# A hybrid decoder step on one core: the V/K stage in eight slices of two K tiles instead of four quarters of four, and four scale-2 weight chunks moved into the first out-projection group

## The chip, the cores and the metric

The kernel runs on one core of one Trainium2 chip. The metric is the device time of one execution in microseconds. Three runs of the kernel before gave 1495.02, 1496.38 and 1498.96 us, median 1496.38.

## The reference, cut to what matters

256 prompt tokens and 8 x 8 sample tokens, 320 in all, D = 2048. All in float32.

```
def mixer_inputs(x, shift, scale, g_pre, w_in, pos):
    h = rms_norm(x, g_pre) * (1.0 + scale) + shift
    z = h @ w_in                       # 2048 -> 4096, columns q | k | v | u
    ...
mp = ada_modulation(c_prompt, ...)     # silu(c) @ w_ada + b_ada -> shift, scale, gate (mixer), shift, scale, gate (MLP)
q, k, v, u = mixer_inputs(xp, mp[0], mp[1], g_pre_mix[l], w_in[l], pos_p)
attn = prompt_attention(q, k, v, pos_p, lam)
pooled = pool_mix(u, ...)
xp = mixer_output(xp, attn, pooled, mp[2], ...)   # x + gate * rms_norm([a | pooled] @ w_out, g_post)
xp = ffn_block(xp, mp[3], mp[4], mp[5], ...)      # the same sandwich around relu(h @ w1)^2 @ w2
```

The sample tokens pass through the same functions with their own modulation (one row for each of 8 sequences), a paged K/V cache of 256 positions and a pooling state.

## The kernel before, in words

Activations lie channel-major: 16 K tiles of 128 channels x 320 tokens. Every weight product is made in three passes of fp32r matmuls (h_hi with w_hi, h_lo with w_hi, h_hi with w_lo): ScalarE rounds a weight half chunk to w_hi (`hi_half`, L390), VectorE subtracts to get w_lo (`lo_half`, L782), TensorE multiplies. A product chunk is 48 matmuls of 128x320.

All weights come as one stream of 272 chunks of 1 MB (128 x 2048 floats), which SP loads in two halves each (L342) into a ring of four slots `raw`. A slot is free again when it has been used: for a product chunk when both halves of w_lo are made, for a modulation ("ada") chunk when its four small matmuls on TensorE (L1500, or L1515 for the later blocks) are done. SP waits for the slots in order, so a late slot also holds up the chunks behind it. The order of the stream and the places of product chunks in it are tables: DENSE has a product at places 2, 5, 8, 11 of 12, SUPER at 1, 3, 5, 7 of 8.

The modulation has 24 blocks of four ada chunks. A block is finished by a copy on ScalarE (`ada_copy`, L384), four transposes on TensorE (`ada_turn`, L1525) and two VectorE steps (`mod_add`, L761 and L764). Blocks 0 to 7 are scale and shift of the mixer, alternating, each for 4 K tiles. Blocks 12 and up are accumulated in parts (`ada_part_chunk`); the first of these parts, blocks 12 to 15, is the scale of the MLP (scale 2), turned by `mod_part`.

The order around the change is written out by hand, engine by engine, with semaphores. At the start TensorE takes block 0, the mean of squares and block 1, while ScalarE and VectorE make rstd, h (scaled, shifted), h_hi and h_lo of the first four K tiles; POOL does the scale and shift of the sample tokens (L1350, L1352). The V/K stage then has four quarters: quarter g multiplies K tiles 4g to 4g+3 with all 16 column tiles of v and k, four tiles to a chunk; each result is the sum over 4 K tiles in one of four PSUM banks, which VectorE adds to v_cm or k_cm (`sum_tiles`, L857). Between them stand the ada chunks of the next two blocks. Then come the Q and U products with attention beside them (`fill`), the sample attention, and the out projection: 16 product chunks, one ada chunk ahead of each (`super4`, L1538), with the evacuation, squares and gates on ScalarE and VectorE. Early in it POOL reloads x (L1443), 2.6 MB. The MLP follows.

## Time and profile before

| what | value |
|---|---|
| median of three runs | 1496.38 us |
| profiled execution | 1494.64 us, its span 1493.0 us |
| TensorE (PE) busy | 1446.6 us, 97% |
| VectorE (DVE) busy | 799.7 us, 54% |
| ScalarE (ACT) busy | 517.5 us, 35% |
| moved by DMA | 316.40 MB, mean 212 GB/s |
| V/K stage | 43.73 to 198.88 us |
| out projection, first product | 410.56 us |

Busy time is the time an engine has an instruction running; matmuls are pipelined, so each is shown as some 310 ns long though a new one starts about every 147. The chain of waits goes back from the last instruction to whatever released each step. PE is the matmul side of TensorE, PEld its weight loads. Times within the span count from its first instruction.

### The profile page before, as it was taken

How to read it: one execution, taken by the hardware profiler on the slowest of the kernel's cores; microseconds unless marked ns; L12 is line 12 of the kernel's file. 1: busy time of each engine (PE TensorE's matmuls, PEld its weight loads, DVE VectorE, ACT ScalarE, POOL GpSimd, SP SyncE). 2: the span in 40 equal slices, each digit the busy share in tenths (PEclk: the TensorE clock that was granted, in tenths of full speed). 3: DMA queues.
4: the chain of work that ended last, by engine and by line, in shares of the span. 5: the costliest groups of instructions: out<-in, count | busy, mean ns of one | idle time of the engine just before them, and what ended most of it. 6: DMA issues, size and time to landing. Idle time of an engine off the chain costs nothing.

```text
span 1493.0 us, 26969 instructions
## 1 busy us (share of the span) xinstructions
PE 1446.6 (97%) x10274; PEld 1313.3 (88%) x10274; DVE 799.7 (54%) x1258; ACT 517.5 (35%) x733; POOL 102.9 (7%) x177
## 2 busy tenths in 40 slices
PE   5999999999899998999999999999999999999996
PEld 1777777778588877999998999999999999999996
DVE  2655558856756568665334444333554344445554
ACT  2222233434456445333322333332333232333331
POOL 1000000067410000000000000000000000000002
PEclk9999999999999999999999999999999999999998
DMA  9999988889687777444445544445544444444431
GB/s 366 345 326 323 325 305 318 284 308 360 226 321 257 258 256 248 141 152 158 143 160 200 176 160 148 147 162 185 192 158 144 157 151 141 143 155 152 141 113 71
DMA packets 87880, 316.40 MB, mean 212 GB/s; under 512 B 12176, under 2 KB 12432, under 8 KB 87168
## 3 DMA queue, kind: packets, MB, share of 16 engines
q1 hardware_dynamic: 79200, 287.87, 56.1%
q0 software_dynamic: 5216, 22.51, 4.1%
q10 hardware_dynamic: 3392, 5.01, 0.9%
q8 instruction: 51, 0.84, 0.2%
q14 instruction: 21, 0.17, 0.0%
HBM read 309.56 MB, written 5.80 MB: 211 GB/s over the span
## 4 chain that ended last, share of the span: by engine, by line
PE 83%; DMA 6%; DVE 3%; POOL 2%; issue 2%; ACT 2%; POOLq 1%; SPq 0%; DVEq 0%; ACTq 0%
PE bank L1538 69%; PE bank L1609 7%; DMA raw<-in_stream 4%; PE bank L1500 3%; PE bank L1515 2%; DMA k_pages<-in_kc 1%; DMA pools_out<-u 1%; DMA pool_w<-in_w_pool 1%; ACT w_hi L390 1%; DVE w_lo L782 1%; PE bank L1861 1%; POOLq L1377 0%; POOL win L1396 0%; POOL win L1398 0%; ACT pair L639 0%
## 5 line engine op out<-in xcount | busy, mean ns | idle before, releaser
L390 ACT ACTIVATE w_hi<-raw 128x1024 fp32r<-128x1024 f32 x352 | 361.8, 1054 | 352.8 <-PE bank L1538 232.8
L782 DVE TENSOR_TENSOR w_lo<-raw,w_hi 128x1024 fp32r<-128x1024 f32 x352 | 419.6, 1225 | 117.1 <-ACT w_hi L390 114.9
L1538 PE MATMUL bank<-m_hi,w_hi 128*128 128x320 f32 x1280 | 397.4, 310 | 1.0 <-issue 0.6
L1538 PE MATMUL bank<-m_hi,w_lo 128*128 128x320 f32 x1280 | 395.5, 309 | 0.0
L1538 PE MATMUL bank<-m_lo,w_hi 128*128 128x320 f32 x1280 | 395.5, 309 | 0.0
L1538 PE MATMUL bank<-h_hi,w_hi 128*128 128x320 f32 x1216 | 379.2, 312 | 0.0
L1538 PE MATMUL bank<-h_hi,w_lo 128*128 128x320 f32 x1216 | 375.7, 309 | 0.0
L1538 PE MATMUL bank<-h_lo,w_hi 128*128 128x320 f32 x1216 | 375.7, 309 | 0.0
L1538 PEld LDWEIGHTS bank<-m_hi,w_hi 128*128 128x128 f32 x1280 | 240.3, 188 | 15.0 <-issue 15.0
L1538 PEld LDWEIGHTS bank<-h_hi,w_hi 128*128 128x128 f32 x1216 | 228.2, 188 | 23.2 <-issue 23.2
L1538 PEld LDWEIGHTS bank<-m_lo,w_hi 128*128 128x128 f32 x1280 | 240.3, 188 | 0.0
L1538 PEld LDWEIGHTS bank<-m_hi,w_lo 128*128 128x128 f32 x1280 | 240.3, 188 | 0.0
L1538 PEld LDWEIGHTS bank<-h_lo,w_hi 128*128 128x128 f32 x1216 | 228.3, 188 | 0.0
L1538 PEld LDWEIGHTS bank<-h_hi,w_lo 128*128 128x128 f32 x1216 | 228.3, 188 | 0.0
L1244 DVE TENSOR_TENSOR relu<-relu 128x320 f32<-128x320 f32 x62 | 30.5, 492 | 191.5 <-ACT relu L672 191.5
L672 ACT ACTIVATE relu<-bank 128x320 f32<-128x320 f32 x60 | 26.2, 437 | 292.4 <-PE bank L1538 292.4
L1259 DVE TENSOR_TENSOR back<-bank,back 128x320 f32 (+1 forms) x48 | 23.6, 491 | 171.7 <-PE bank L1538 171.7
L1609 PE MATMUL bank<-h_hi,w_hi 128*128 x256 | 83.0, 324 | 1.4 <-DVE v_cm L857 0.6
L1609 PE MATMUL bank<-h_hi,w_lo 128*128 x256 | 79.1, 309 | 0.0
L1609 PE MATMUL bank<-h_lo,w_hi 128*128 x256 | 79.0, 309 | 0.0
L1609 PEld LDWEIGHTS bank<-h_hi,w_hi 128*128 128x128 f32 x256 | 48.0, 188 | 29.4 <-issue 24.2
L1464 POOL TENSOR_TENSOR back<-back,rstd 128x640 f32<-128x640 f32 (+1 forms) x3 | 3.9, 1314 | 938.1 <-ACT rstd L715 938.1
(237 smaller groups left out, 1095.3 us busy)
## 6 DMA issues: line engine op xcount, KB each, us to landing
raw<-in_stream SPq DMA_DIRECT2D x544, 512.0 KB, 5.0
k_pages<-in_kc POOLq DMA_DIRECT2D x16, 512.0 KB, 9.3
v_pages<-in_vc POOLq DMA_DIRECT2D x16, 512.0 KB, 6.9
x<-in_x_cm ACTq DMA_DIRECT2D x1, 2560.0 KB, 12.2
x<-in_x_cm POOLq DMA_DIRECT2D x1, 2560.0 KB, 10.8
v_out<-v_cm POOLq DMA_DIRECT2D x1, 1280.0 KB, 9.5
k_out<-back POOLq DMA_DIRECT2D x1, 1280.0 KB, 10.2
y_out<-x SPq DMA_DIRECT2D x2, 640.0 KB, 3.0
```

Of the source, the lines that this page charges most:

```text
L390: act.activation(w_hi[2 * (j % 2) + h][:, :], raw[slot][:, h * 1024:(h + 1) * 1024], ACT.Copy).then_inc(hi_ready, 1)
L672: freed(act.activation(relu[j % 2][:, :], bank[j % 2][:, 0:T], ACT.Relu), j)
L782: dve.tensor_tensor(w_lo[q][:, :], raw[slot][:, h * 1024:(h + 1) * 1024], w_hi[q][:, :], ALU.subtract).then_inc(slot_used[slot], 1)
L1244: mine.then(dve.tensor_tensor(relu2[j % 2][:, :], up, up, ALU.mult))
L1259: dve.tensor_tensor(tile, bank[j % 2][:, 0:T], tile, ALU.add).then_inc(bank_free[j % 2], 1)
L1464: mine.then(pool.tensor_tensor(part, part, rstd[:, :].unsqueeze(1).to_broadcast([P, end - first, T]), ALU.mult))
L1500: last = pe.matmul(ADA[32 * kk:32 * kk + NSEQ, :], silu_c[:, 4 * a + kk, :], raw[slot][:, kk * 512:(kk + 1) * 512], start=(a == 0), stop=( ...
L1515: last = pe.matmul(ADA[32 * g:32 * g + NSEQ, :], silu_c[:, a, :], raw[slot][:, g * 512:(g + 1) * 512], start=start, stop=(a == KT - 1))
L1538: last = pe.matmul(bank[j % 2][:, 0:T], w[q][:, k * P:(k + 1) * P], v[:, 8 * h + k, :], start=(h == 0 and k == 0 and n == 0), stop=(h == 1 ...
L1609: last = pe.matmul(QUARTER_BANKS[2 * h + i][:, 0:T], w[q][:, (4 * i + k) * P:(4 * i + k + 1) * P], v[:, ds(4 * g + k, 1), :].rearrange("p ...
L1861: last = pe.matmul(FIRST_BANKS[i][:, 0:T], w[q][:, at_k:at_k + P], v[:, 4 * c + k, :], start=(c == 0 and k == 0 and n == 0), stop=(c == 3 ...
```

## The change

The V/K stage runs in 8 slices of two K tiles instead of 4 quarters of four. A product chunk now holds 2 K tiles of 8 column tiles, so each half chunk writes all four PSUM banks with sums over two K tiles, and VectorE adds 128 such sums instead of 64. An ada block 0 to 7 now holds the scale and the shift of the same two K tiles, so one block (four chunks) is enough for a slice; the place table is SLICED, with products at 0, 3, 6, 9 of 12. ScalarE applies scale and shift to the prompt tokens in one instruction for each K tile, where VectorE used two. x is loaded on SP's queue, in four parts ahead of the stream, instead of ScalarE's; the squares, the sums and their mean stand ahead of block 0 on TensorE. The ten `keep_clock` matmuls are gone. The stream begins with 4 ada chunks instead of 8; everything up to the out projection moves up by four ada chunks, and the first out-projection group takes 8 of them (DENSE): the last four of scale 2 and the first four of shift 2. `make_scale2` therefore stands behind the first out-projection evacuation on VectorE.

```diff
-STREAM = 8 + 12 * QUARTERS + 12 * Q_GROUPS + 8 * (U_GROUPS + OUT_GROUPS) + 36 * GROUPS
+SLICES = 2 * QUARTERS
+STREAM = 4 + 12 * (QUARTERS + Q_GROUPS + 1) + 8 * (U_GROUPS + OUT_GROUPS - 1) + 36 * GROUPS
+SLICED = [0, 3, 6, 9]
+SLICED_ADA = [[1, 2, 4, 5], [7, 8, 10, 11]]
 DENSE = [2, 5, 8, 11]
-DENSE_ADA = [[0, 1, 3, 4], [6, 7, 9, 10]]
+NORMED = [(0, 2), (2, 4), (4, 8), (8, 12), (12, 16)]
 SUPER = [1, 3, 5, 7]
...
     def quarter_use(g):
-        return 2 + 3 * g
+        return 1 + 3 * g
 
     def out_use(n):
-        return 2 + 3 * (QUARTERS + Q_GROUPS) + 2 * (U_GROUPS + n)
+        return quarter_use(QUARTERS + Q_GROUPS) + 2 * (U_GROUPS + n) + (1 if n else 0)
 
...
+        for g in range(4):
+            sp.dma_start(x[:, 4 * g:4 * g + 4, :], x_cm[:, 4 * g:4 * g + 4, :]).then_inc(x_loaded[g], 16)
...
-        act.dma_start(x[:, :, :], x_cm).then_inc(x_loaded, 16)
...
+        def slice_h(n):
+
+            act.wait_ge(gate_done, n + 1)
+            act.wait_ge(normed_s, normed_by(n))
+            act.wait_ge(mod_done, n + 2)
+            for k in range(2):
+                tile = normed[:, 2 * n + k, 0:NP_]
+                act.activation(tile, tile, ACT.Identity, bias=mod[:, n, 2 + k, 0:1], scale=gate[:, 2 * n + k, 0:1]).then_inc(
+                    prompt_mod, 1)
+            act.wait_ge(prompt_mod, 2 * n + 2)
+            act.wait_ge(sample_mod, n + 1)
+            act.activation(h_hi[:, 2 * n:2 * n + 2, :], normed[:, 2 * n:2 * n + 2, :], ACT.Copy).then_inc(h_hi_s, 1)
...
-        ada_copy(1, 1, 3)
+        hi_half(0, quarter_use(0), SLICED[0], 0, 0)
+        slice_h(0)
+        hi_half(0, quarter_use(0), SLICED[0], 0, 1)
...
+        for n in range(SLICES):
+            second, following = slice_chunks(n)
+            for h in range(2):
+                hi_half(*second, h)
+            ada_copy(n + 1, quarter_use(n // 2), SLICED_ADA[n % 2][3])
+            hi_half(*following, 0)
+            if n + 1 < SLICES:
+                slice_h(n + 1)
+            hi_half(*following, 1)
...
+        def slice_gate(n):
+
+            mod_add(n)
+            dve.wait_ge(mod_done, n + 2)
+            dve.scalar_tensor_tensor(gate[:, 2 * n:2 * n + 2, :], mod[:, n, 0:2, :], 1.0,
+                                     gain[:, G_PRE_MIX + 2 * n:G_PRE_MIX + 2 * n + 2].unsqueeze(2).to_broadcast([P, 2, NSEQ]),
                                      ALU.add, ALU.mult).then_inc(gate_done, 1)
...
         invert_root(0)
-        mod_add(0)
-        times_rstd(normed, x, 0).then_inc(normed_s, 1)
-        dve.wait_ge(normed_s, 1)
-        dve.wait_ge(mod_done, 2)
-        scale_quarter(0)
-        mod_add(1)
-        shift_quarter(0)
-        low_of_h(1, 0)
-        for h in range(2):
-            lo_half(0, quarter_use(0), DENSE[0], 0, h)
-        for g in range(1, 4):
-            times_rstd(normed, x, g).then_inc(normed_s, 1)
-        dve.wait_ge(normed_s, 4)
+        for first, end in NORMED[:3]:
+            times_rstd(first, end)
+        slice_gate(0)
+        lo_half(0, quarter_use(0), SLICED[0], 0, 0)
+        low_of_h(0)
+        lo_half(0, quarter_use(0), SLICED[0], 0, 1)
+        for first, end in NORMED[3:]:
+            times_rstd(first, end)
...
+        def sum_tiles(n, jj, h):
+            half = 4 * n + 2 * jj + h
+            for i in range(4):
+                if i < 3:
+                    dve.wait_ge(first_done, 3 * half + i + 1)
                 else:
+                    dve.wait_ge(half_free, half + 5)
+                tile = (v_cm, k_cm)[jj][:, 4 * h + i, :]
+                dve.tensor_tensor(tile, QUARTER_BANKS[i][:, 0:T], tile, ALU.add).then_inc(bank_free[i], 1)
...
+        for n in range(SLICES):
+            second, following = slice_chunks(n)
+            for h in range(2):
+                lo_half(*second, h)
+                sum_tiles(n, 0, h)
+            if n + 1 < SLICES:
+                slice_gate(n + 1)
+            else:
+                mod_add(n + 1)
+            lo_half(*following, 0)
+            sum_tiles(n, 1, 0)
+            if n + 1 < SLICES:
+                low_of_h(n + 1)
+            lo_half(*following, 1)
+            sum_tiles(n, 1, 1)
...
+        def make_scale2():
+            mod_part(0, out_use(0), DENSE[1] - 1)
+            dve.wait_ge(part_done, 1)
+            dve.scalar_tensor_tensor(scale2[:, :, :], mod_of(SCALE2), 1.0,
+                                     gain[:, G_PRE_FFN:G_PRE_FFN + KT].unsqueeze(2).to_broadcast([P, KT, NSEQ]),
+                                     ALU.add, ALU.mult).then_inc(gate_done, 1)
...
+                if 4 * t + j == 1:
+                    make_scale2()
...
+        def quarter(g, last):
             use = quarter_use(g)
-            for j in range(4):
-                if j:
-                    second_ada(g, use, j)
-                else:
-                    pe.wait_ge(h_ready, g + 1)
-                slot, u = use_of(use, DENSE[j])
-                for h in range(2):
-                    pe.wait_ge(slot_used[slot], 2 * u + (3 + h))
-                    q = 2 * (j % 2) + h
-                    for i in range(2):
-                        pe.wait_ge(bank_free[2 * h + i], 4 * g + (j + 1))
-                        for k in range(4):
-                            for n, (w, v) in enumerate(((w_hi, h_hi), (w_hi, h_lo), (w_lo, h_hi))):
-                                last = pe.matmul(QUARTER_BANKS[2 * h + i][:, 0:T], w[q][:, (4 * i + k) * P:(4 * i + k + 1) * P],
-                                                 v[:, ds(4 * g + k, 1), :].rearrange("p a t -> p (a t)"),
-                                                 start=(k == 0 and n == 0), stop=(k == 3 and n == 2))
-                        last.then_inc(half_free if i else first_done, 1)
-                        if j == 3 and h == 0 and i == 0:
-                            ada_turn(3 + 2 * g)
-                        if j == 3 and h == 1 and i == 0:
-                            second_ada(g + 1, use + 3, 0)
-                    if h == 0 and j < 3:
-                        first_ada(g, use, j + 1)
-                    elif h == 0:
-                        first_ada(g + 1, use + 3, 0)
-                if j == 1:
-                    ada_turn(2 + 2 * g)
+
+            def slice_tiles(i, jj, h, tiles):
+
+                j = 2 * i + jj
+                slot, u = use_of(use, SLICED[j])
+                q = 2 * (j % 2) + h
+                pe.wait_ge(slot_used[slot], 2 * u + (3 + h))
+                for b in tiles:
+                    pe.wait_ge(bank_free[b], 8 * g + (2 * j + h + 1))
+                    for k in range(2):
+                        for n, (w, v) in enumerate(((w_hi, h_hi), (w_hi, h_lo), (w_lo, h_hi))):
+                            last = pe.matmul(QUARTER_BANKS[b][:, 0:T], w[q][:, (2 * b + k) * P:(2 * b + k + 1) * P],
+                                             v[:, ds(4 * g + (2 * i + k), 1), :].rearrange("p a t -> p (a t)"),
+                                             start=(k == 0 and n == 0), stop=(k == 1 and n == 2))
+                    last.then_inc(first_done if b < 3 else half_free, 1)
+
+            for i in range(2):
+                nb, places = 2 * g + (i + 1), SLICED_ADA[i]
+                ada_chunk(nb, use, places[0], 0)
+                pe.wait_ge(h_ready, 2 * g + (i + 1))
+                slice_tiles(i, 0, 0, range(4))
+                ada_chunk(nb, use, places[1], 1)
+                ada_chunk(nb, use, places[2], 2)
+                slice_tiles(i, 0, 1, range(2))
+                ada_chunk(nb, use, places[3], 3)
+                slice_tiles(i, 0, 1, range(2, 4))
+                ada_turn(nb)
+                slice_tiles(i, 1, 0, range(4))
+                slice_tiles(i, 1, 1, range(2))
+                if last and i == 1:
+                    nb, place, a = fill_ada(0)[0][0]
+                    ada_chunk(nb, fill(0)[1], place, a)
+                slice_tiles(i, 1, 1, range(2, 4))
+
+        with pe.Fori(0, QUARTERS - 1) as g:
+            quarter(g, False)
+        quarter(QUARTERS - 1, True)
...
-        for t in range(OUT_GROUPS - 1):
+        for j in range(4):
+            for i in range(2):
+                k = 2 * j + i
+                ada_part_chunk(k // 4, out_use(0), DENSE[j] - 2 + i, (12 + k) % KT, k == 4)
+            for h in range(2):
+                product_half(*out_chunk(j), h, m_hi, m_lo, mix_wait)
+        for t in range(1, OUT_GROUPS - 1):
             super4(OUT_C4 + t, out_use(t), 1, 4 * t, m_hi, m_lo, mix_wait)
```

Three places in the order of the instructions. First TensorE, from the start up to the first product; raw are ada chunks, the number being the slot of the ring (49 to 52), squares and rstd belong to the mean. Before:

```order
L1500 MATMUL bank<-raw_52,silu_c 9x512 x4
L1485 MATMUL bank<-rstd,ones 128x320
L1525 MATMUL bank<-tab,ada_rows 128x128 x4
L1500 MATMUL bank<-raw_49,silu_c 9x512 x4
L1500 MATMUL bank<-raw_50,silu_c 9x512 x4
L1500 MATMUL bank<-raw_51,silu_c 9x512 x4
L1500 MATMUL bank<-raw_52,silu_c 9x512 x4
L1525 MATMUL bank<-tab,ada_rows 128x128 x4
L1500 MATMUL bank<-raw_49,silu_c 9x512 x4
L1500 MATMUL bank<-raw_50,silu_c 9x512 x4
L1490 MATMUL bank<-ones 128x128 x10
```

and now, up to the waits in front of the first product:

```order
L1486 MATMUL bank<-squares,ones 32x320 x16
L1493 MATMUL bank<-rstd,ones 128x320
L1508 MATMUL bank<-raw_49,silu_c 9x512 x4
L1508 MATMUL bank<-raw_50,silu_c 9x512 x4
L1508 MATMUL bank<-raw_51,silu_c 9x512 x4
L1508 MATMUL bank<-raw_52,silu_c 9x512 x4
L1533 MATMUL bank<-tab,ada_rows 128x128 x4
L1620 UNCONDITIONAL_BRANCH
L1620 ISA
L1507 ISA
L1508 MATMUL bank<-raw_50,silu_c 9x512 x4
L1605 REGISTER_ALU
```

Of the ten ada chunks in front of the first product five are left (four of block 0, one of block 1), and the mean stands first.

Second VectorE in the V/K stage; w_lo is half a product chunk, v_cm and back (its upper half is k_cm) take the sums. Before, from the second half of a quarter:

```order
L782 TENSOR_TENSOR w_lo_59<-raw_52,w_hi_55 128x1024
L782 TENSOR_TENSOR w_lo_60<-raw_52,w_hi_56 128x1024
L857 TENSOR_TENSOR back<-bank,back 128x320
L854 REGISTER_ALU
L857 TENSOR_TENSOR back<-bank,back 128x320 x2
L854 REGISTER_ALU
L857 TENSOR_TENSOR back<-bank,back 128x320
L815 ISA x2
L815 SCALAR_TENSOR_TENSOR gate<-mod,gain 128x36
L818 REGISTER_ALU
L820 ISA
L820 TENSOR_TENSOR normed<-normed,gate 128x4x256
```

and now, the first slice:

```order
L806 TENSOR_TENSOR w_lo_59<-raw_52,w_hi_55 128x1024
L864 TENSOR_TENSOR v_cm<-bank,v_cm 128x320 x4
L806 TENSOR_TENSOR w_lo_60<-raw_52,w_hi_56 128x1024
L864 TENSOR_TENSOR v_cm<-bank,v_cm 128x320 x4
L785 TENSOR_REDUCE mod<-bank 128x36
L788 TENSOR_TENSOR mod<-mod,ada_bias 128x36
L834 SCALAR_TENSOR_TENSOR gate<-mod,gain 128x18
L806 TENSOR_TENSOR w_lo_57<-raw_51,w_hi_53 128x1024
L864 TENSOR_TENSOR back<-bank,back 128x320 x4
L827 TENSOR_TENSOR h_lo<-normed,h_hi 128x640
L806 TENSOR_TENSOR w_lo_58<-raw_51,w_hi_54 128x1024
L864 TENSOR_TENSOR back<-bank,back 128x320 x4
```

Four sums stand behind each half of w_lo where two stood, and w_lo halves alternate with them; the two VectorE steps on normed in each quarter are gone.

Third TensorE where the out projection begins; u and pool_w belong to the pooling mixer, m_hi is the input of the out projection. Before:

```order
L1727 MATMUL bank<-back,ones 128x512
L1744 MATMUL bank<-u,pool_w 128x320 x12
L1515 MATMUL bank<-raw_49,silu_c 9x512 x4
L1538 MATMUL bank<-m_hi,w_hi_53 128x320
L1538 MATMUL bank<-m_lo,w_hi_53 128x320
L1538 MATMUL bank<-m_hi,w_lo_57 128x320
```

and now:

```order
L1727 MATMUL bank<-back,ones 128x512
L1744 MATMUL bank<-u,pool_w 128x320 x12
L1523 MATMUL bank<-raw_49,silu_c 9x512 x4
L1523 MATMUL bank<-raw_50,silu_c 9x512 x4
L1546 MATMUL bank<-m_hi,w_hi_53 128x320
L1546 MATMUL bank<-m_lo,w_hi_53 128x320
L1546 MATMUL bank<-m_hi,w_lo_57 128x320
```

Two ada chunks stand ahead of the first product chunk, which is the third chunk of its group instead of the second.

## Rows read from the trace of the kernel before

**Rows 1.** The page: busy time of TensorE, and the chain that ended last.
```profile
PE 1446.6 (97%) x10274; PEld 1313.3 (88%) x10274; DVE 799.7 (54%) x1258; ACT 517.5 (35%) x733; POOL 102.9 (7%) x177
...
PE 83%; DMA 6%; DVE 3%; POOL 2%; issue 2%; ACT 2%; POOLq 1%; SPq 0%; DVEq 0%; ACTq 0%
```

**Rows 2.** Stretches: length, busy us of each engine, granted clock, DMA share, GB/s.
```profile
0.00:20.00 20.00, 7.84 (x20) 1.07 (x22) 3.41 (x26) 6.53 (x7) 3.26 (x7) 1.00 0.87 328
20.00:43.70 23.70, 18.42 (x126) 6.73 (x122) 10.04 (x12) 6.71 (x8) 5.65 (x3) 1.00 1.03 409
...
43.73:198.88 155.15, 154.24 (x1058) 120.23 (x1059) 86.41 (x126) 41.86 (x43) 4.43 (x7) 1.00 0.94 327
```

**Rows 3.** Timeline 0 to 44 us: start, length, engine, line, what [idle before].
```profile
8.37 1.88 PE L1500 MATMUL bank<-raw,silu_c 128*9 128x512 f32 x4
...
8.47 0.17 ACT L364 ACTIVATE small<-bank 128x2 f32<-128x2 f32 x1 [2.50 <-PE bank L1563]
14.14 4.75 ACT L369 ACTIVATE squares<-x 128x1280 f32<-128x1280 f32 x4 [5.50 <-DMA x<-in_x_cm]
...
23.00 0.60 PE L1500 MATMUL bank<-raw,silu_c 128*9 128x512 f32 x2
...
23.84 0.44 ACT L373 ACTIVATE rstd<-bank 128x320 f32<-128x320 f32 x1 [4.95 <-PE bank L1478]
...
26.15 2.15 DVE L750 RECIPROCAL rstd<-rstd 128x320 f32<-128x320 f32 x1 [6.15 <-ACT rstd L378]
...
29.50 1.03 PE L1500 MATMUL bank<-raw,silu_c 128*9 128x512 f32 x4 [0.25 <-DMA raw<-in_stream]
...
35.76 0.60 ACT L384 ACTIVATE ada_rows<-bank 128x512 f32<-128x512 f32 x1 [9.15 <-PE bank L1500]
...
37.44 0.20 DVE L764 TENSOR_TENSOR mod<-mod,ada_bias 128x36 f32<-128x36 f32 x1
...
39.56 1.27 ACT L420 ACTIVATE h_hi<-normed 128x1280 fp32r<-128x1280 f32 x1 [3.20 <-POOL normed L1352]
...
40.86 1.49 DVE L809 TENSOR_TENSOR h_lo<-normed,h_hi 128x1280 fp32r<-128x1280 f32 x1 [1.96 <-ACT h_hi L420]
41.05 1.06 ACT L390 ACTIVATE w_hi<-raw 128x1024 fp32r<-128x1024 f32 x1 [0.22 <-DMA raw<-in_stream]
...
43.73 0.41 PE L1609 MATMUL bank<-h_hi,w_hi 128*128 x1 [0.47 <-DVE w_lo L782]
```

**Rows 4.** Timeline of POOL: one step beside VectorE, and the same step later.
```profile
30.59 1.74 POOL L1350 TENSOR_TENSOR normed<-normed,gate 128x256 f32<-128x256 f32 x1 [2.91 <-DVE gate L815]
...
73.96 0.72 POOL L1350 TENSOR_TENSOR normed<-normed,gate 128x256 f32<-128x256 f32 x1 [34.49 <-DVE gate L815]
```

**Rows 5.** Chain of waits, 80 to 125 us: start, length, what.
```profile
87.59 3.72 PE bank L1609 x24
91.30 0.97 PE bank L1500 x8
...
102.81 5.92 DMA raw<-in_stream
```

**Rows 6.** Chain of waits, 405 to 445 us, out projection.
```profile
410.56 7.27 PE bank L1538 x48
...
418.81 7.24 PE bank L1538 x48
```

**Rows 7.** Groups of the V/K stage: busy us, mean ns | idle before.
```profile
L782 DVE TENSOR_TENSOR w_lo<-raw,w_hi 128x1024 fp32r<-128x1024 f32 x32 | 39.1, 1224 | 59.0 <-ACT w_hi L390 58.8
...
L857 DVE TENSOR_TENSOR v_cm<-bank,v_cm 128x320 f32<-128x320 f32 x32 | 13.4, 480 | 0.0
```

**Rows 8.** Out projection: POOL's reload of x, SP's issues at 411.5, ScalarE's next w_hi.
```profile
409.85 0.60 POOL L1443 DMA_DIRECT2D x<-in_x_cm  x1 [9.61 <-issue]
...
L342 SPq DMA_DIRECT2D raw<-in_stream x2: 353/548/744, 411.5 to 412.4; - x2
...
423.56 1.06 ACT L390 ACTIVATE w_hi<-raw 128x1024 fp32r<-128x1024 f32 x1 [3.50 <-DMA raw<-in_stream]
```

More of the change, by code:

```diff
@@ L60 @@
 FFN_C4 = OUT_C4 + OUT_GROUPS
-BANK_LEAD = 4 * QUARTERS - 2 * Q_C4
+BANK_LEAD = 8 * QUARTERS - 2 * Q_C4
 U_ORDER = [6, 7, 4, 5, 2, 3, 0, 1]
@@ new lines, in times_rstd @@
+        def times_rstd(first, end):
+            dve.tensor_tensor(normed[:, first:end, :], x[:, first:end, :],
+                              rstd[:, :].unsqueeze(1).to_broadcast([P, end - first, T]), ALU.mult).then_inc(normed_s, 1)
+        invert_root(0)
+        for first, end in NORMED[:3]:
[6 more added lines that the diff above has]
+            times_rstd(first, end)
```

236 lines of the change are left out of this document (88 added, 148 removed).

## The prediction

> **What bounds the kernel now.** I read the page first, then busy time by stretch, the timeline of the first 44 us, the groups of lines of the V/K stage, and the chain of waits in that stage and in the out projection. TensorE is busy 97% of the span and is 83% of the chain that ended last [rows 1]. So time is won where TensorE stands idle, and lost where it gets more work or a new wait. In the stretch 20.00 to 43.70 the DMA engines are full at 409 GB/s; in the V/K stage, 43.73 to 198.88, TensorE is busy 154.24 of 155.15 us [rows 2]. So there are two regimes: a start in which TensorE waits for bytes and for the chain that makes h, and a stage in which it hardly waits at all (0.91 us).
>
> The start, step by step [rows 3]: ScalarE squares x from 14.14 to 18.89; the last half chunk of scale-and-shift block 0 lands at 23.00; the rstd chain (copy 23.84, square root, reciprocal) ends at 28.30; block 1 (the shift) is through TensorE only at 35.76; its values are in at 37.64; h_hi ends at 40.83, h_lo at 42.35; the first product chunk lands at 41.05, and the first product starts at 43.73, after its w_lo. The product needs both 8 modulation chunks and the eleventh chunk of the stream.
>
> **The start after the change.** Bytes first. x now goes first on SP's queue. The row at 29.50 [rows 3] is TensorE waiting for the first half of stream chunk 6 (counted from 0), so x, the tables and chunks 0 to 5 had landed one half chunk earlier: 0.524 MB at 409 GB/s is 1.28 us, so at 28.2. The same bytes are ahead of chunk 5 now. SP's first DMA waited for VectorE's memset before and x does not, which is worth up to 0.9 us: I place chunk 5 at about 27.4 and its four TensorE matmuls' end at 28.0. Chunk 3 comes at 22.2 instead of 23.0.
>
> The h chain: ScalarE is free at 8.64 and the four squares take 4.75 [rows 3], x lands by about 11, so they end at 13.4. Sums add about 0.9, and from copy to reciprocal it is 4.46 (23.84 to 28.30): 18.8. The first three times_rstd cover 2560 elements, at the 1.49 of 1280 that h_lo shows 3.0: 21.8, before block 0 is through. Block 0: the second half of chunk 3 at 22.2, ada matmuls 0.7, then copy, turn and mod_add 1.93 (35.71 to 37.64): 24.9, gate 0.25: 25.1. Then two ScalarE activations of 256 (0.45 each by the h_hi row's rate plus start-up), beside two POOL operations of half the size of the ones in [rows 4]; they cost 0.4 to 0.9 each, I take 1.5 for the pair: 26.6. h_hi of 640 is half of 1.27, h_lo half of 1.49: with starts 28.2. Both paths meet at about 28.2. I take 28.5 for the first product; ends 27 and 31. Gain **15.2** (12.7 to 16.7).
>
> A rule of the Trainium skill bears on the POOL pair: "SBUF — State Buffer", section "SBUF: two separate sides", says that GpSimd and VectorE's instructions with two SBUF inputs take one port pair in turns, the later one blocked for the whole instruction. Rows agree: the same POOL operation took 1.74 us started right behind a VectorE one, 0.72 otherwise [rows 4]. By it the pair waits behind w_lo (VectorE, 1.22) and the start would be 29.3, the gain 0.8 smaller; by the undisturbed rows it would be 27.9.
>
> **V/K stage.** TensorE's product work is the same: 768 matmuls, 16 chunks. Half chunks of 24 take 3.72 followed by 0.97 for an ada chunk [rows 5]; 48 in one piece take 7.24 [rows 6]; so 24 more matmuls are 3.52 and each change of kind costs 0.2. Before, 32 ada chunks stood singly; now a slice of two products has three groups (1, 2 and 1), so 8 changes fewer, −1.6. Between first product and first Q product there were 32 ada chunks, now 33 (31 of blocks 1 to 8 and 2 of block 9): +1.0. A slice is then 4x3.52+4x0.98+3x0.2+0.4 (turn) = 19.0 us.
>
> VectorE is the new risk. Each slice has 16 sums of 128x320 instead of 8 per two products: 16x0.48 and 4 w_lo x1.22 [rows 7], mod_add and gate 0.7, h_lo 0.75: 14.0 of 19.0 us. With a 0.2 wake-up for each sum it is 17.2. It holds; four banks take turns, a bank is wanted 2.6 us after its last matmul. The chain turn, mod_add, gate, two activations, h_hi, h_lo ends about 5 us after the turn, and TensorE has 7.2 us of the second product left: hidden with 2 us spare. The cost of sums if that cover is gone is in the rivals.
>
> The ring of four slots: chunks 0 and 3 of a slice are products, whose slot frees with the second w_lo. A second half issued at 102.81 landed at 108.73 [rows 5]; it leaves about 0.6 after the slot is free, and a first half lands 1.28 before it. So from a free slot it is about 5.2 us to the first half and 6.6 to the second. In a later slice the second w_lo ends about 1.3 before the slice's end, its successor lands 5.3 after the slice starts and is wanted at 5.6: zero waiting, barely. In the first slice VectorE makes the second w_lo at 29.6 (after h_lo), so chunk 8 lands at 36.3 and its matmuls end at 36.8; TensorE wants it at 28.5+3.7+1.0 = 33.2 and would be done at 34.2: a wait of **2.6**. The stage before had waits of 0.9. Sum of the stage: +1.0−1.6+2.6−0.9 = **+1.1** (0 to +8).
>
> Q and U stages: the same chunks in the same pattern, starting 14.1 us earlier; attention, POOL's pages and stores hang on the stage, not on the clock on the wall. 0 (−2 to +2).
>
> **Out projection.** Four ada chunks more stand in group 0: 4x0.98 = 3.9. Before, TensorE finished the only ada chunk ahead of the first product at 410.2 and began at 410.56, after m_lo [rows 6]; the second now fills that: 3.9−0.35 = **+3.6**. VectorE's make_scale2 (transpose, add, scale) moves behind the first evacuation: some 2 us of VectorE beside a 9.2 us product tile, hidden.
>
> The new wait: the pattern before was ada, product, ada, product, and the four slots held both first products when the stage began. Now it is ada, ada, product, ada, and the second product is chunk 5, whose slot frees only when the second ada chunk is used (411.3). At that moment POOL reloads the 2.6 MB of x (issued 409.85), and the chunk issued at the same time before, at 411.5, was readable by ScalarE only at 423.56 [rows 8]: 12 us. w_hi 1.06 and w_lo 1.22 make it 425.8. TensorE is ready at 411.3+7.2+0.2+1.95 = 420.8. Wait **+5.0** (0 to +6). Before, that landing hit the third product and cost nothing.
>
> **Sum:** −15.2+1.1+3.6+5.0 = −5.5. The profiled execution took 1494.64 (span 1493.0), the median of the runs is 1496.38, 1.7 above it; so 1489.1 on the profiled one's scale and **1490.9** as a median.
>
> **Rivals.** (a) The late second product costs nothing: x and the stream share differently and chunk 5 lands 5 us earlier. For it: 4.7 MB at 409 GB/s needs 11.5, so against it. −10.5: 1485.9.
> (b) VectorE, not TensorE, sets the V/K slices. For: 128 sums instead of 64, each between a TensorE finish and a bank that TensorE wants back, with w_lo and mod_add in front of them in program order. Against: 14.0 of 19.0. It is even at 0.7 us a slice (5.5/8); at 1.4 a slice (bank waits of 0.35 at each of the four halves) it costs 11.2: 1502.1, slower.
> (c) The ring runs late in every slice, since the margin is 0.3: about 1 us in 7 slices, +7: 1497.9. For: raw landings are what ScalarE waits for in this stage already; against: the load per slice is 15.4 of 19.0 us.
> (d) The start comes out at half rate. The first four records of an ada chunk take 1.88, those at 29.50 take 1.03 [rows 3], and the granted clock reads 1.00 in both stretches [rows 2], so only durations show that the early ones ran near half the rate (1.2 against 2.4 GHz), after a start without work. Between 22.9 and 28.2 TensorE would be busy about 2.1 of 5.3 us (half of chunk 3, a turn, chunk 5), less than in any stretch before, and the ten keep_clock matmuls are gone. The first half product would then take 7 instead of 3.5; 2.6 of that hides in the wait for chunk 8; the rest, and what follows at the low level, costs up to 4: 1494.9.
> The Trainium skill, "TensorE: Matmul & The Clock Gate", section "HAM oscillation — how this bites in real kernels", names this danger: too little matmul work puts the array back to half clock. By it the time is that of (d), without it that of the sum; the rows at the start of the trace agree that a low level exists.
>
> **Chances.** Forecast 0.45; (a) 0.15; (b) 0.12; (c) 0.13; (d) 0.15. 0.3% is 4.5 us, about what a measurement of this kernel tells from no change, so the line runs at 1491.9, close above the forecast. Six tenths of the forecast (0.27), (a) (0.15) and a piece of (c) and (d) where they cost almost nothing (0.07) are faster: 0.49. Same: the rest of the forecast (0.18), most of (d) (0.11) and part of (c) (0.07): 0.36. Slower, above 1500.9: (b) and the tail of (c): 0.15. Range 1484 to 1499.5, which leaves out the worst of (b) and little of (a).
>
> **What would show it.** First product at 28.5 in the timeline; a TensorE wait on the stream of about 2.6 us at 33 to 37; slices of 19.0 us with no VectorE sum as releaser; first Q product near 184.8; in the out projection a wait of 5 us before the second product with w_lo as releaser; x_scaled unchanged beside it. Wrong would be: waits on sums in every slice, first product after 31, or no wait at the second out product.

## The result, and the profile after

The changed kernel took 1508.91 us (median of 4 runs, 1503.69 to 1513.10) against 1496.18 us for the kernel before, a ratio of 1.0074 (95% interval 1.0043 to 1.0105). A second set of 9 runs gave 1507.49 us and 1.0065 (1.0049 to 1.0081). So it is slower by 0.7%, 10 to 13 us, where 5.5 us of gain were forecast, and outside the forecast's range. The profiled execution took 1503.69 us with a span of 1502.0 us, 9.05 us more than the profiled one of the kernel before. It is the fastest of its four runs, and the profiled one of the second set (1511.04 us) the slowest of its nine, so the two profiles stand at the two ends of what this kernel does.

The page of the changed kernel, busy time and the chain that ended last, answers to [rows 1]:

```profile
PE 1447.3 (96%) x10254; PEld 1314.2 (87%) x10254; DVE 816.2 (54%) x1323; ACT 526.2 (35%) x753; POOL 108.6 (7%) x185
...
PE 82%; DMA 6%; DVE 4%; POOL 2%; issue 2%; ACT 2%; POOLq 1%; SPq 1%; ACTq 0%; DVEq 0%
```

TensorE has 0.7 us more work and the span is 9.0 us longer: the loss is idle time, and the page doesn't say where. Stretches of the changed kernel do, with the columns of [rows 2]; the cuts are the first V/K product, the wait in the last V/K step and the first Q product:

```profile
20.00:30.68 10.68, 7.07 (x29) 0.86 (x21) 6.86 (x10) 4.43 (x6) 1.90 (x2) 0.78 1.00 362
30.68:181.30 150.62, 150.41 (x1026) 118.77 (x1024) 100.76 (x182) 48.40 (x59) 13.04 (x15) 0.99 0.93 331
181.30:192.56 11.26, 7.37 (x41) 4.31 (x40) 5.79 (x10) 2.11 (x2) 0.00 (x0) 0.85 0.47 167
192.56:384.00 191.44, 184.17 (x1662) 144.93 (x1658) 124.52 (x286) 73.12 (x161) 65.38 (x126) 1.00 0.89 316
```

For 150 us of the V/K stage TensorE stands still for 0.2 us; in the next 11 us it loses 3.9, and the granted clock is 0.85 there. The timeline of that place (start, length, engine, line, what, and in brackets the idle time before it with what ended it):

```profile
182.34 1.06 ACT L403 ACTIVATE w_hi<-raw 128x1024 fp32r<-128x1024 f32 x1 [6.28 <-DMA raw<-in_stream]
183.43 1.23 DVE L806 TENSOR_TENSOR w_lo<-raw,w_hi 128x1024 fp32r<-128x1024 f32 x1 [5.07 <-ACT w_hi L403]
...
184.57 1.68 DVE L864 TENSOR_TENSOR back<-bank,back 128x320 f32<-128x320 f32 x4
185.20 0.38 PE L1597 MATMUL bank<-h_hi,w_hi 128*128 128x320 f32 x1 [3.90 <-DVE back L864]
...
187.64 1.90 PE L1508 MATMUL bank<-raw,silu_c 128*9 128x512 f32 x8
...
192.56 0.41 PE L1546 MATMUL bank<-h_hi,w_hi 128*128 128x320 f32 x1
```

Read it upwards. TensorE waits for a bank that VectorE must sum (L864). VectorE stood idle 5.07 us in front of a w_lo (L806) that comes ahead of those sums in its program: it belongs to the first Q chunk, which landed only at 182.34. The ada chunk behind it (one chunk is eight records) then took 1.90 us, against 1.05 for the one at 191.59: the granted clock reads 0.50 from 187.6 to 189.6.

The same picture 200 us later, timeline of the last pair of the sample attention:

```profile
384.71 1.06 ACT L403 ACTIVATE w_hi<-raw 128x1024 fp32r<-128x1024 f32 x1 [11.31 <-DMA raw<-in_stream]
385.67 0.51 ACT L561 ACTIVATE dprobs<-bank,small 128x320 f32<-128x320 f32 x1
385.80 1.23 DVE L806 TENSOR_TENSOR w_lo<-raw,w_hi 128x1024 fp32r<-128x1024 f32 x1 [7.92 <-ACT w_hi L403]
...
386.97 0.35 ACTq L572 DMA_DIRECT2D pool_w<-in_w_pool  x1
...
388.14 0.69 PE L1757 MATMUL bank<-tab,dprobs 128*128 128x128 f32 x2 [7.06 <-DVE dprobs L1022]
```

The chunk of the first out product lands at 384.7, 26 us before that product needs it, but the softmax of the last pair (L561, L1022) and the transfer of the pool weights (L572) stand behind its cast and its subtract. TensorE idles for 7.1 us, and the lead of 6.2 us is gone.

The third place is the out projection, where the chain of waits answers to [rows 6] (start, length, what; "issue" is time for which the chain names nothing that TensorE waited for, x16 at L1523 are two ada chunks):

```profile
410.38 11.29 DMA raw<-in_stream
...
424.87 1.91 issue
426.78 7.28 PE bank L1546 x48
434.06 1.83 PE bank L1523 x16
435.89 7.24 PE bank L1546 x48
```

The second product starts 15.8 us after the first (8.25 before). Timeline of ScalarE and VectorE, which answers to [rows 8]:

```profile
424.29 1.06 ACT L403 ACTIVATE w_hi<-raw 128x1024 fp32r<-128x1024 f32 x1 [14.54 <-DMA raw<-in_stream]
...
425.45 2.38 DVE L806 TENSOR_TENSOR w_lo<-raw,w_hi 128x1024 fp32r<-128x1024 f32 x2 [13.16 <-ACT w_hi L403]
```

The chunk could be read at 424.29 (423.56 before, where the third product took it), and the product starts when the first half of its w_lo is done, so the 1.91 us of "issue" are a wait for it. In the profile of the second set that product also ran slowly; its chain, and the stretch it lies in:

```profile
428.96 1.90 issue
430.86 9.99 PE bank L1546 x48
```

```profile
430.00:436.00 6.00, 5.14 (x19) 5.17 (x20) 3.86 (x8) 2.46 (x5) 1.17 (x2) 0.50 1.03 410
```

48 matmuls took 9.99 us instead of 7.28, at a granted clock of 0.50, the lower of the two levels (1.2 GHz).

Here is each profile by stage, in us. "attention" holds the Q and U products and both attentions. The cuts are the first V/K product, the first Q product, the first pooling product, the first out product and the first product of the MLP; behind the last cut all of them are within 0.2 us of each other.

```
                        start   V/K   attention  pooling  out    MLP starts
before                  43.7   155.0   199.0     12.9    142.1   552.7
changed                 30.7   161.9   205.0     13.4    150.9   561.9
changed, second set     29.1   165.6   207.1     13.3    154.2   569.3
forecast of the change -15.2    +1.1     0        +8.6 with out  -5.5
changed - before       -13.0    +6.9    +6.0     +0.5     +8.8    +9.2
second set - before    -14.6   +10.6    +8.1     +0.4    +12.1   +16.6
```

### The profile page after: what moved, and what is told of

Read it like the earlier page. It is cut to its first block, busy times and chain, and to the rows that moved or that the text cites. A ratio compares the mean times of both kernels' runs of the same rounds, so it can differ in the third digit from the quotient of the medians.

```text
span 1502.0 us, 26900 instructions
## 1 busy us (share of the span) xinstructions
PE 1447.3 (96%) x10254; PEld 1314.2 (87%) x10254; DVE 816.2 (54%) x1323; ACT 526.2 (35%) x753; POOL 108.6 (7%) x185
## 4 chain that ended last, share of the span: by engine, by line
PE 82%; DMA 6%; DVE 4%; POOL 2%; issue 2%; ACT 2%; POOLq 1%; SPq 1%; ACTq 0%; DVEq 0%
PE bank L1546 67%; PE bank L1597 7%; DMA raw<-in_stream 4%; PE bank L1508 2%; PE bank L1523 2%; DMA k_pages<-in_kc 1%; DVE w_lo L806 1%; DMA pools_out<-u 1%; ACT w_hi L403 1%; POOL win L1404 0%; ACT pair L667 0%; POOLq L1385 0%; DVE pair L1208 0%; SPq L356 0%; ACT h_hi L671 0%
## 5 line engine op out<-in xcount | busy, mean ns | idle before, releaser
L806 DVE TENSOR_TENSOR w_lo<-raw,w_hi 128x1024 fp32r<-128x1024 f32 x352 | 419.6, 1224 | 96.1 <-ACT w_hi L403 95.0
L1597 PE MATMUL bank<-h_hi,w_hi 128*128 (+1 forms) x256 | 83.3, 325 | 3.9 <-DVE back L864 3.9
L1597 PE MATMUL bank<-h_hi,w_lo 128*128 (+1 forms) x256 | 79.7, 311 | 0.0
L1597 PE MATMUL bank<-h_lo,w_hi 128*128 (+1 forms) x256 | 79.6, 311 | 0.0
```

The source lines that it names most:

```text
L806: dve.tensor_tensor(w_lo[q][:, :], raw[slot][:, h * 1024:(h + 1) * 1024], w_hi[q][:, :], ALU.subtract).then_inc(slot_used[slot], 1)
L1597: last = pe.matmul(QUARTER_BANKS[b][:, 0:T], w[q][:, (2 * b + k) * P:(2 * b + k + 1) * P], v[:, ds(4 * g + (2 * i + k), 1), :].rearrange(" ...
```

## The experiments

Each kernel is the changed one with the edit shown ("..." marks what is left out of an edit or a view); where it has more than one, the text says so. The runs were taken in three sets, in which the kernel before had medians of 1497.32, 1494.98 and 1497.51 us. Each ratio is to that kernel in the same set. The first set holds the changed kernel again and the next three experiments, the second the four from "the first two chunks" to "three scale-2 chunks", the third the rest. A difference in us between kernels of two sets is uncertain by those 2.5 us.

**The changed kernel again.**

> The changed kernel once more, as the base for the runs beside it. Its four times lay between 1503.69 and 1513.10 us. If that spread is the kernel's own (another phase of the weight ring against the waits), it shows again: a median of 1504 to 1513 and a profile whose first Q product starts near 192.6 and whose second out product starts near 426.8. If it was the chip, the runs agree within 4 us. The ratio to the kernel before is 1.004 to 1.011 in both.

Measured: 1507.49 us, 1506.02 to 1511.04: a spread of 5 us for the 9.4 of the first four runs. The profiled execution is at the upper end (1511.04 us). So the spread is neither that of the first four nor within the 4 us of the other reading. Its first Q product is at 194.7 and its second out product at 430.86, each 2 to 4 us later than in the first profile. The three places are the same. What differs: the first Q chunk landed 9.8 us after its issue instead of 8.4, TensorE waited 2.3 us for pages of K at 378.7, and the product behind the wait in the out projection ran at the lower clock.

**Sums first in the last V/K step.**

```
+            if n == SLICES - 1:
+                sum_tiles(n, 1, 0)
+                sum_tiles(n, 1, 1)
+                lo_half(*following, 0)
+                lo_half(*following, 1)
+                continue
...
```

> In the last V/K step alone VectorE sums its eight banks before it subtracts the halves of the first Q chunk. Theory A (the first Q chunk sits at place 2 of its group, its slot comes free only at 172.4, and VectorE's sums stand behind its late subtract): TensorE's gap at 181.3 to 185.2 goes, the first Q product starts at about 188 in place of 192.6, and the lead over the kernel before is some 10 us there. Theory B (the ring itself is behind at the end of the stage, so the wait only moves to the first Q product's weights): the first Q product starts at 191 to 193. In both the end of the kernel moves little as long as the wait at the end of the sample attention stands: theory A1 (that wait hangs on a slot which a TensorE step frees, so it moves with TensorE) says the whole 4 us come through, about 1500; theory A2 (it ends by a transfer whose time is set elsewhere) says 0 to 1 us come through.

Measured: 1504.13 us, ratio 1.0043 (1.0020 to 1.0065), 3.4 us under the changed kernel. The V/K stage takes 158.1 us against 161.9 and 165.6, and the first Q product starts at 187.2. Timeline of that place:

```profile
182.57 0.49 DVE L864 TENSOR_TENSOR back<-bank,back 128x320 f32<-128x320 f32 x1 [0.39 <-PE bank L1602]
182.86 1.06 ACT L403 ACTIVATE w_hi<-raw 128x1024 fp32r<-128x1024 f32 x1 [7.32 <-DMA raw<-in_stream]
...
185.92 2.35 DVE L806 TENSOR_TENSOR w_lo<-raw,w_hi 128x1024 fp32r<-128x1024 f32 x2
```

The chunk is no earlier (182.86), yet nothing stands behind it, and TensorE waits nowhere for a sum. Theory A holds, B falls. The wait in the sample attention is still 7.3 us, so it moved along with TensorE (A1) rather than eating the gain. The 1500 us of the expectation were counted from the first profile's 1503.69; against the nine runs beside it, 3.4 of the 4 us came through.

**First out product at place 1.**

```
+EARLY = [1, 5, 8, 11]
+EARLY_ADA = [[0], [2, 3, 4], [6, 7], [9, 10]]
...
-        return OUT_C4 + n // 4, out_use(n // 4), (SUPER if n // 4 else DENSE)[n % 4], n % 4
+        return OUT_C4 + n // 4, out_use(n // 4), (SUPER if n // 4 else EARLY)[n % 4], n % 4
...
```

TensorE's order and the stream's order follow the same table.

> In the first out-projection group alone the first product goes to place 1 of the group (the places become 1, 5, 8, 11), as in the kernel before; its scale-2 and shift-2 chunks keep their order. Theory A (the first out product's chunk came late because its slot 2 is freed by the last U group's third adaptive chunk at 377.4): ScalarE's 11.3 us and VectorE's 7.9 us idle before 384.7 and TensorE's 7.1 us before 388.1 go, the pool weight transfer is issued at about 381.5, the pooling products start at 391 to 392 in place of 397.7, and the kernel ends about 6 us earlier: 1497 to 1499 in the profile. The wait before the second out product stays (4 to 6 us). Theory B (the cover for it is the page loads, and the chunk comes late whatever its place): no change, 1503 to 1509.

Measured: 1500.89 us, ratio 1.0029 (1.0006 to 1.0051), 6.6 us under the changed kernel. Timeline of the same two lines as above:

```profile
377.56 1.06 ACT L405 ACTIVATE w_hi<-raw 128x1024 fp32r<-128x1024 f32 x1 [1.97 <-DMA raw<-in_stream]
379.36 0.53 ACT L563 ACTIVATE dprobs<-bank,small 128x320 f32<-128x320 f32 x1 [0.75 <-DVE small L1016]
```

(The expectation calls the freeing chunk the group's third; it is its fourth and last, at place 6.) ScalarE's idle time went from 11.31 to 1.97 us, and the attention stage takes 197.2 us against 205.0 and 207.1. Theory A. The pooling products start at 393.2, not at 391 to 392: they wait 1.7 us for the pool weights.

**Only the order changed: cast and subtract behind the softmax.**

```
-            hi_fill(fills[0] + 1, 0)                 # and (.., 1), lo_fill alike
+            if pr < 3:
+                hi_fill(fills[0] + 1, 0)
...
                 attn_hi(slice(0, 4), slice(0, NP_), 2)
+                for h in range(2):
+                    hi_fill(fills[0] + 1, h)
```

> The places stay as in the changed kernel; only the cast and the subtract of the first out product's chunk are issued behind the softmax steps of the last sample pair, on ScalarE and on VectorE, so that nothing stands behind them. Theory A (the loss at the end of the sample attention is the order on the two engines, the steps queued behind a late chunk): the 7.1 us gap of TensorE before 388.1 goes although the chunk lands as late as before, and the kernel gains 5 to 6.5 us. Theory B (the late chunk itself is what the first out product needs): it lands at 384.7, 26 us before that product starts at 411, so by this theory the gain is nothing only if the steps behind did not matter: 0 to 1 us.

Measured: 1502.42 us, ratio 1.0035 (1.0012 to 1.0059), 5.1 us less. Timeline, the softmax turn on TensorE and the chunk:

```profile
381.38 0.38 PE L1766 MATMUL bank<-tab,dprobs 128*128 128x128 f32 x2
...
386.18 1.06 ACT L403 ACTIVATE w_hi<-raw 128x1024 fp32r<-128x1024 f32 x1 [3.15 <-DMA raw<-in_stream]
```

The chunk is 1.5 us later than in the changed kernel and the 7.1 us gap is gone all the same: attention 198.6 us. So what costs is the work queued behind a late chunk, and its lateness alone costs nothing here, 26 us ahead of its product. Some of it comes back in the pooling stage (15.8 us for 13.4), where both engines now have the cast and the subtract to do.

**The first two chunks of the out group used 20 us earlier.**

```
             if pr == 3:
                 fill_half(fills[0], 1)
+                for k in range(2):
+                    ada_part_chunk(0, out_use(0), k, 12 + k, False)
```

> The places stay as in the changed kernel; TensorE uses the first two chunks of the out group (places 0 and 1) about 20 us earlier, right after the last half of the sixteenth fill product, while the transfers would otherwise stand still (the DMA share is 0.05 and less from 392 to 408). So the chunks at places 4 and 5 load ahead of the x reload. Theory A (the wait before the second out product, 421 to 427, is the late release of slots 0 and 1 at 410, beside the x reload): the wait goes, and with it the fall of the granted clock that made that product 10.0 us in place of 7.3 in one of two profiles; the two chunks' 2.1 us of TensorE leave the end of the group for the attention. The kernel gains 6 to 9 us: 1498 to 1501 against 1507.5. Theory B (the stream has too little reserve there whatever is released early: 12 chunks for 4 products): the wait moves to the third or fourth product, and the gain is 0 to 3 us.

Measured: 1501.99 us, ratio 1.0028 (1.0000 to 1.0056), 5.5 us less by the medians of two sets and by the ratios, just short of A's 6 to 9. The chain of waits in the out group:

```profile
415.94 7.27 PE bank L1546 x48
...
425.04 7.23 PE bank L1546 x48
432.27 1.83 PE bank L1523 x16
434.11 0.24 issue
434.35 7.27 PE bank L1546 x48
```

The second product follows the first by 9.1 us, as its two ada chunks say, at full clock. The stage takes 144.4 us for 150.9 and 154.2; 1.8 us of that are the two chunks themselves, which the attention now holds (208.4 us for 205.0 and 207.1). Theory A; the waits that moved on are 0.24 and 0.53 us, so B is nearly nothing.

**The reload of x 4 us later.**

```
+        pool.wait_ge(half_free, 8 * OUT_C4 + 5)
         pool.dma_start(x[:, :, :], x_cm).then_inc(x_again, 16)
```

> GpSimd reloads x only once the first half of the first out product is done (about 4 us later); nothing else changes. Theory A (the chunk at place 4 takes 11 to 12 us from its issue because it shares the queues with the x reload; alone it takes 7): it lands some 4 us earlier, the second out product starts 4 us earlier (11.7 us after the first in place of 15.7), and the clock falls in fewer runs: 1502 to 1505 against 1507.5. Theory B (what is late is the release of its slot, and the chunk would be late by itself): the gain is under 1 us. A loss would show where x is read first, in the squares of x during the third product.

Measured: 1505.51 us, ratio 1.0064 (1.0041 to 1.0087): 2.0 us less by the medians, which is less than the sets differ by, and no difference by the ratios (1.0065). So no gain is shown, and neither theory as it stood. The chain of waits:

```profile
422.37 10.92 DMA raw<-in_stream
...
434.36 2.64 issue
437.00 8.81 PE bank L1547 x48
```

The second product came 10.0 us after the first, so the chunk of place 4 was indeed late because of the reload; but the wait went to the third product, at 437.00 for 435.89, whose chunk now took 10.9 us beside x. Bytes that must pass in this stretch were moved, and the loss with them.

**The two edits together.**

> The sums ahead of the late chunk in the last V/K step, and the first out product at place 1: the two edits that were run alone. Theory A (two separate losses in series, 6.6 us by the medians of the profiles and about 6 to 7 us): they add up, with the out group as it was: 1494 to 1498, the first out product at about 400 to 402. Theory A' (the pool weights' transfer, issued by ScalarE behind the first half of the sixteenth fill product, is then what the pooling products wait for): 2 to 3 us of it stay behind: 1497 to 1500. Theory B (a later common wait swallows the lead): no better than either alone, 1501.

Measured: 1498.38 us, ratio 1.0029 (1.0005 to 1.0053). V/K 160.4, attention 198.8, first out product at 400.9, without a wait of over 1 us for the pool weights: by the stages both gains are there (A). By the times they are not shown to add up: the ratio is that of the first out product at place 1 alone (1.0029), and the 2.5 us between the two medians are about what the sets differ by. The out stage takes 155.0 us, with the second product at the lower clock:

```profile
417.10 10.00 PE bank L1553 x48
```

**Both, and three scale-2 chunks used early.**

```
+                ada_part_chunk(0, out_use(0), 0, 12, False)     # behind the sixteenth fill product
...
         mix_pool(1)
+        for k in (1, 2):
+            ada_part_chunk(0, out_use(0), k + 1, 12 + k, False)
```

> Both edits, and the first three scale-2 chunks of the out group used by TensorE within the sample attention and between the pooling products (place 0 behind the sixteenth fill product, places 2 and 3 behind the second pooling product), so that the chunks of places 4 to 7 load while the transfers would stand still. Theory A (three losses, all of them slots that are released late): all waits of TensorE over 1 us from 180 to 450 go, the granted clock stays at 1.00 there, and the kernel ends at 1484 to 1490, faster than the kernel before. Theory B (the out group's twelve chunks are more than the stream can bring beside the products): a wait stays in the group, 1492 to 1497.

Measured: 1487.18 us, ratio 0.9938 (0.9920 to 0.9955); again, in the last set, 1485.89 us and 0.9922 (0.9895 to 0.9949). This is faster than the kernel before by 0.6 to 0.8%, and than the changed one by some 20 us. The chain of waits:

```profile
402.85 7.28 PE bank L1553 x48
...
411.11 7.24 PE bank L1553 x48
418.34 1.83 PE bank L1530 x16
420.18 7.24 PE bank L1553 x48
```

The first three products follow each other without a wait; the stage takes 143.2 us (three of its ada chunks, some 2.8 us, now stand ahead of it). The expectation had no wait over 1 us; five are left between 180 and 450, of 1.26 to 2.23 us, all in the attention or right before the first out product. One of them is of a kind that the kernel before doesn't show: 1.31 us for the pages of V at 386.55, beside a stream that now loads there.

**Only one chunk used early.**

> Both edits, and of the scale-2 chunks only the one at place 0 used early (behind the sixteenth fill product); those at places 2 and 3 stay behind the first out product. Theory A (the wait before the second product hangs on slots 0 and 1 alone, which the first out product and this one chunk release early): no wait over 1 us before the second product, 1487 to 1490 as with three early chunks; the pooling products run 2 us shorter and the out group 2 us longer. Theory B (the reserve of a whole round of the ring is what counts): the wait moves to the third product, 1 to 4 us long, 1490 to 1494.

Measured: 1491.27 us, ratio 0.9956 (0.9940 to 0.9973), 5.4 us above the three early chunks in the same set. The chain of waits:

```profile
418.73 2.06 PE bank L1530 x16
420.80 3.12 issue
423.92 8.71 PE bank L1553 x48
```

Theory B: the second product is on time (411.50), the third waits 3.1 us and then runs at 8.71 for 7.24 us. So the number of chunks already in the slots counts, and not only those of the second product.

**TensorE kept busy in the wait.**

```
                 k = 2 * j + i
+                if j == 1:
+                    keep_clock(bank[7], 10)
...
+            if j == 1:
+                keep_clock(bank[7], 8)
```

> The changed kernel with 10 small products of a constant tile with itself ahead of each of the two adaptive chunks before the second out product and 8 more ahead of that product; their result is read by nobody. The wait for the chunk stays, TensorE is merely busy in it. Theory A (half of what this wait costs is the granted clock that falls in it: the second out product took 7.3 us in one profile and 10.0 in another): the clock stays at 1.00 from 418 to 440, the product takes 7.3 us in every profile, the spread of the times narrows and the median falls by 1 to 3 us to 1505 to 1506. Theory B (the clock has no part in it): no change, 1507.5, or 1 to 2 us more, for the 28 products themselves where they outlast the wait.

Measured: 1507.35 us, ratio 1.0057 (1.0034 to 1.0081). The chain of waits:

```profile
426.76 1.98 PE bank L1498 x16
428.74 7.23 PE bank L1546 x48
```

The clock reads 1.00 throughout and the product takes 7.23 us, as theory A says of the mechanism: the 34.0 us from the first out product to the fourth were 37.8 in the profile of the changed kernel's second set (34.6 in the first). The median didn't follow (0.1 us less than in another set, with intervals that overlap almost wholly), and the spread did not narrow (6.5 us for 5.0), so what it is worth over many runs stays open.

**TensorE kept busy at the start.** Ten such products behind the first transpose, on top of the kernel with three early chunks.

> The same with 10 small products of a constant tile on TensorE behind the first transpose of the adaptive rows (as the kernel before had them there), so that it is not idle from 24.4 to 27. Theory A (the first step starts at the lower clock: in the changed kernel's first profile the chunks of 26.7 and 28.9 took 1.9 us in place of 1.0 and the first product came at 30.7 in place of 28.5): the clock is 1.00 from 24 to 36, the first product starts at 28.8 to 29.3, and the gain is 0.5 to 1.5 us. Theory B (the first product waits for the chain of h and for the chunk's transfer, which the clock does not move): no change beyond 0.5 us.

> The kernel with both edits and three early chunks once more, as the base for the runs beside it: 1487 us, ratio 0.992 to 0.996 to the kernel before, first Q product at 188, first out product at 403, with no fall of the clock from 180 to 450.

Measured: 1486.44 us with them and 1485.89 without, ratios 0.9924 and 0.9922. The stretch 24 to 28 us, first without them, then with:

```profile
24.00:28.00 4.00, 1.12 (x7) 0.13 (x5) 2.35 (x5) 3.06 (x5) 1.74 (x2) 0.73 1.00 334
```

```profile
24.00:28.00 4.00, 3.42 (x26) 2.30 (x24) 2.36 (x5) 3.10 (x5) 1.75 (x2) 1.00 1.00 353
```

The clock holds, the first product starts at 29.7 instead of 30.6, and the time is the same: theory B by the time. Nine profiles without these products had the ada chunk ahead of the first product (place 1) at 25.4 to 26.0. Seven of them kept the clock at 1.00 and started at 28.8 to 29.4; in the other two it read 0.67 and 0.76 from 24 to 28 us, and they started at 28.9 and 29.1 all the same. The three that had it at 26.7 to 27.1 read 0.73 to 0.77 and started at 29.9 to 30.7.

## Why the prediction was wrong, point by point

**The start, −15.2: right in mechanism, 0.6 to 2.2 too large.** Measured −13.0 and −14.6. The chunk that bounds it was read at 26.68 and 28.86 in the changed kernel's first profile:

```profile
26.68 1.88 PE L1508 MATMUL bank<-raw,silu_c 128*9 128x512 f32 x4 [2.25 <-DMA raw<-in_stream]
28.14 0.83 DVE L827 TENSOR_TENSOR h_lo<-normed,h_hi 128x640 fp32r<-128x640 f32 x1 [1.69 <-ACT h_hi L438]
28.86 1.88 PE L1508 MATMUL bank<-raw,silu_c 128*9 128x512 f32 x4 [0.30 <-DMA raw<-in_stream]
30.68 0.64 PE L1597 MATMUL bank<-h_hi,w_hi 128*128 x1
```

I had its end at 28.0. The h chain was forecast to end at 28.2 and ended at 28.97; in the second set's profile, where the chunk came earlier, that chain set the start at 29.07. What was too small in it is POOL's pair, put at 1.5 us: its first step, beside VectorE's w_lo, took 1.44 us and the second 0.46, and they were through at 27.27 for 26.6. That is the other reading that the prediction gave of this pair, with a start at 29.3. Rival (d), the start at half rate, came true in the first profile, for 1 us or so, and not in all of them. The section "HAM oscillation — how this bites in real kernels" of "TensorE: Matmul & The Clock Gate" in the Trainium skill has waits that put the array back to the low level so that the next work starts cold; the trace agrees here (1.88 us for 1.03 at 28.86) and, more dearly, in the out projection of the second set's profile (9.99 for 7.28 us).

**V/K stage, +1.1: this is the first step that failed.** Seven steps went as forecast: a period of 19.27 us for 19.0 (the turns in the second set, 43.02 to 177.93), no wait for a sum, no late ring; the wait for chunk 8 was 0.2 to 1.9 for 2.6. With the last step mended the stage is +3.1 (158.1 measured), of which 7 x 0.27 is 1.9. So rivals (b) and (c) were wrong. But I worked out one step and took eight of it. In the last one the chunk that follows is not at place 0 of its group but the Q chunk at place 2, cast and subtracted in the same program positions although it lands only at 182.34; the kernel before had the sums of one half ahead of it there. That cost 3.8 us in the first profile and 7.5 in the second, with the lower clock behind the wait in it.

**Q and U stages and the attention, "the same chunks in the same pattern", 0 (−2 to +2): the step that failed most, +6.0 and +8.1.** The stages themselves kept their pattern; their last fill doesn't belong to them. It is the first out product, and the change moved it from place 1 to place 2 of its group, from a slot that a w_lo frees to one freed by the last ada chunk of the second U group, at 377.4. I wrote of this edit only where its product is used, in the out projection, and never asked which instructions of the sample attention stand behind its cast. Two experiments, one on the place and one on the order, each took the loss away.

**Out projection, +3.6 and the new wait +5.0: right, and then too small.** The second product was forecast 14.5 us after the first (411.3 to 425.8; the prediction's terms for when TensorE is ready add up to 420.65, not 420.8) and came 15.8 after it, by the reason given: slots released at 410 beside the reload of x. That it started at 426.78, near the 425.8, is chance: the forecast's 425.8 is a time of the kernel before, without the lead of 14 us that it had forecast, and the two losses ahead had used up the lead that there was. The stage cost +8.8 in one profile and +12.1 in the other. What I left out is that such a wait is paid twice: the clock falls, and the product behind it took 8.6 to 10.0 us instead of 7.3 in seven of the eight profiles that have an unfilled wait before the second or the third product. In the eighth, the first profile, the ada chunk within the wait paid (3.15 us, clock 0.50), and the clock was back before the product.

**The sum.** −13.0 +6.9 +6.0 +0.5 +8.8 = +9.2 up to the MLP. The forecast's terms had −5.5. The failed steps are the 0 for the Q and U stages and the attention, and the last slice within the +1.1 of the V/K stage; the rest is a start 0.6 to 2.2 us too hopeful and an out projection 0.2 to 3.5 us too cheap. None of the rivals was it: (b) and (c) put the danger in a repeated step, (a) in the out projection and (d) at the start, and both misses lie at a seam, where one stage's code handles the next stage's first chunk.

## What to carry to other kernels

When a ring of buffers or the places in a group change, walk each in-order queue across every seam: for each chunk, when is its slot released, and which instructions of another stage stand behind the first one that reads it. A late transfer costs what is queued behind its first reader, and can be mended by order alone (5.1 of some 10 us here), by place, or by using cheap chunks early while the transfers stand idle. Price a wait of TensorE at its length and the slower product after it.

## What the runs showed of the hardware

- A product of 48 matmuls took 7.23 to 7.28 us at a granted clock of 1.00 and 8.63 to 10.00 where TensorE had stood idle for 3.1 to 4.6 us in all ahead of it (once it took 7.28 all the same); with small products in the wait it took 7.23.
- From 392 to 408 us the DMA engines were at a share of 0.06 or less in the changed kernel, just ahead of a group of twelve chunks; SP's next issue came at 410.2, when the first two of them were used. Three chunks used earlier in that gap were worth 11 us (1498.38 to 1487.18).
- A half chunk of 512 KB took 10.9 to 12.0 us from its issue beside the 2.6 MB reload of x, and 8.4 and 9.8 us in the last V/K step (issued at 173.91 and 174.47 in the two profiles of the changed kernel), where nothing but the stream was loading. Moving the reload only chose which chunk pays.
- Times of the kernel before on one chip lay between 1490.9 and 1508.9 us, wider than the three runs first shown (1495.02 to 1498.96): the stage lengths of a profile told kernels apart that single times did not.
